# An RWKV pass: lora's second products as 64-row tiles in one place, y in one bank, turn steps at full width, normalisation in the next scan

## The reference, cut to what matters

```python
h = jnp.concatenate([x, dx], axis=-1) @ w_comb
r, k, v, g, w_lo, a_lo = jnp.split(h, ...)            # 2048 wide each; w_lo and a_lo are 64 wide
w = -jax.nn.softplus(-(w0 + jnp.tanh(w_lo) @ w2)) - 0.5
a = jax.nn.sigmoid(a0 + a_lo @ a2)
...
y = _wkv7_scan(r, decay, k, v, -kk, kk * a)           # a recurrence over tokens, a 64 x 64 state per head
mean, var = ...                                       # of y, over a head's 64
y = ((y - mean) * lax.rsqrt(var + GN_EPS)).reshape(B, L, D_INNER)
y = y * ln_w + ln_b
y = (y + bonus) * jax.nn.silu(g)
return y @ w_out
```

## Time and profile before

| | us |
|---|---|
| three runs | 2237.74, 2241.88, 2242.10 (median 2241.88) |
| the profiled execution | 2238.95 |
| its span in the profile | 2237.2 |
| passes 0 to 17 on PE | from about 753 to about 1680 |
| one full pass (scan to scan) | 54.23 |

### The profile page before, as it was taken

How to read it: one execution, slowest core, us unless ns; L and a number is a source line. 1 busy time by engine, 2 the same in 40 slices (tenths; PEclk the granted TensorE clock), 3 DMA queues, 4 the chain that set the end, 5 groups by cost and what they waited for, 6 DMA issues and landing times.

```text
span 2237.2 us, 51106 instructions
## 1 busy us (share of the span) xinstructions
PE 2205.0 (99%) x21595; PEld 1783.4 (80%) x21595; DVE 1262.2 (56%) x2442; ACT 838.3 (37%) x1725; POOL 1156.3 (52%) x802
## 2 busy tenths in 40 slices
PE   8999999999999999999999999999999999999998
PEld 7888888788888677777777777777789788888877
DVE  5465467877730955555555555656550376656621
ACT  4122212333310445555555555555421334434311
POOL 5555567787766263444444444444636444444454
PEclk9999999999999999999999999999999999999999
DMA  3323233333332222222222222222523332212132
GB/s 117 95 76 85 76 95 94 94 95 96 103 105 85 63 84 60 70 80 70 70 80 79 80 72 70 70 72 79 188 62 100 111 79 64 60 48 64 53 131 85
DMA packets 262107, 188.02 MB, mean 84 GB/s; under 512 B 18283, under 2 KB 242409, under 8 KB 261497
## 3 DMA queue, kind: packets, MB, share of 16 engines
q1 hardware_dynamic: 261881, 184.76, 27.6%
HBM read 162.69 MB, written 22.04 MB: 83 GB/s over the span
## 4 chain that ended last, share of the span: by engine, by line
PE 93%; DVE 3%; POOL 1%; ACT 1%; issue 1%; DMA 0%; SPq 0%; DVEq 0%; POOLq 0%; ACTq 0%
PE ps L1415 21%; PE ps L161 16%; PE ps L162 15%; PE ps L163 15%; PE ps L1601 3%; PE ps L1617 3%; PE ps L1643 2%; PE ps L1590 2%; PE ps L2561 1%; PE ps L1428 1%; PE ps L1557 1%; PE ps L226 1%; PE ps L1529 1%; PE ps L1546 1%; PE ps L1579 1%; PE ps L1515 1%
## 5 line engine op out<-in xcount | busy, mean ns | idle before, releaser
L152 POOL TENSOR_TENSOR w_lo<-raw,w_hi 128x1024 fp32r<-128x1024 f32 (+1 forms) x164 | 418.7, 2553 | 13.7
L149 POOL TENSOR_SCALAR w_hi<-raw 128x1024 fp32r<-128x1024 f32 (+1 forms) x164 | 182.8, 1114 | 438.8 <-PE ps L163 424.1
L161 PE MATMUL ps<-h_hi,w_hi 128*128 128x512 f32 x616 | 243.0, 395 | 4.0 <-DVE h_lo L936 2.3
L163 PE MATMUL ps<-h_hi,w_lo 128*128 128x512 f32 x616 | 240.9, 391 | 0.0
L162 PE MATMUL ps<-h_lo,w_hi 128*128 128x512 f32 x616 | 240.8, 391 | 0.0
L1415 PE MATMUL ps<-mixed_k,raw 128*64 128x264 f32 x1024 | 149.3, 387 | 0.0
L1415 PE MATMUL ps<-mixed_r,raw 128*64 128x264 f32 x1024 | 143.9, 387 | 0.0
L161 PEld LDWEIGHTS ps<-h_hi,w_hi 128*128 128x128 f32 x616 | 116.4, 189 | 29.3 <-DVE h_lo L1119 2.8
L1415 PE MATMUL ps<-mixed_g,raw 128*64 128x264 f32 x1024 | 138.3, 386 | 0.0
L163 PEld LDWEIGHTS ps<-h_hi,w_lo 128*128 128x128 f32 x616 | 116.2, 189 | 24.8
L162 PEld LDWEIGHTS ps<-h_lo,w_hi 128*128 128x128 f32 x616 | 116.4, 189 | 23.2
(11 more groups left out here) (477 smaller groups left out, 6008.5 us busy)
## 6 DMA issues: line engine op xcount, KB each, us to landing
raw<-in_rwkv_w_in_dram SPq DMA_DIRECT2D x64, 512.0 KB, 4.1
raw<-in_w_up_dram SPq DMA_DIRECT2D x44, 512.0 KB, 3.8
raw<-in_w_in_dram SPq DMA_DIRECT2D x41, 512.0 KB, 3.9
raw<-in_w_down_dram SPq DMA_DIRECT2D x22, 512.0 KB, 3.6
raw<-in_mla_w_in_dram SPq DMA_DIRECT2D x22, 512.0 KB, 4.0
sb_kept<-xT SPq DMA_DIRECT2D x16, 528.0 KB, 2.7
xT<-sb_kept SPq DMA_DIRECT2D x16, 528.0 KB, 4.7
raw<-in_rwkv_w_out_dram SPq DMA_DIRECT2D x16, 512.0 KB, 3.6
```

The source lines that it names most:

```text
L149: nc.gpsimd.tensor_scalar(w_hi[s][:, 0:width], raw[s][:, 0:width], 1.0, 0.0, ALU.mult, ALU.add).then_inc(split_hi, 1)
L152: nc.gpsimd.tensor_tensor(w_lo[s][:, 0:width], raw[s][:, 0:width], w_hi[s][:, 0:width].bitcast(F32), ALU.subtract).then_inc(split_ready, 1)
L161: nc.tensor.matmul(dst, w[0], x[0], start=start, stop=False)
L163: return nc.tensor.matmul(dst, w[1], x[0], start=False, stop=stop)
```

## The change

1. **Lora.** `wz` becomes `wa_rows`, 128 x 128: w's 64 rows above a's. Two memsets on DVE go. A new `lora_products` makes all four products in one piece, w0, a0, w1, a1, each one product on a 64-row tile, into banks 1, 7, 4 and 6 (from column 64). It is one step, the fourth of a pass (after `LORA_LEAD` = 3 steps of r0; in pass 0 after 7), and waits for the last `a_ev` of the pass before and for the bonus's eviction. `ITEMS` has w0, a0, w1, a1 first. There are 64 + 1 steps.
2. **Fills.** `FILL_END` is 0, the first chunk's fills are (1, 2, 1). In chunk 0 the first fill runs before the wait for `tl_ev`, not behind the products of line 1538.
3. **y** of chunks 0 to 7 lies in bank 5, of chunk 8 in bank 6; ACT evicts 512 and 64 columns where it had 256 and 320.
4. **Turn.** The two steps of `FILL_TURN` are one product each over the array's full width (`wide`).
5. **Normalisation.** For passes 2 to 14 (`deferred`) DVE's multiplication is cut in two halves and moved into chunk 1 of the next pass's scan, ACT's `gn_affine` behind its items of chunk 2. z and its write follow; SP's `load_sums` goes behind the load of v's weights.

```diff
-wz = raw[0][:, KD * P:KD * P + 2 * P].rearrange("p (a b) -> p a b", a=2)
+wa_rows = raw[0][:, KD * P:KD * P + P]
...
-SCAN_FILLS = [(1, 2, 2)] + [(1, 1, 2)] * (NC_ - 2) + [(1, 1, 2)]
-FILL_TURN, FILL_GRAM, FILL_FIRST, FILL_END = 2, 7, 4, 2
+SCAN_FILLS = [(1, 2, 1)] + [(1, 1, 2)] * (NC_ - 1)
+FILL_TURN, FILL_GRAM, FILL_FIRST, FILL_END = 2, 7, 4, 0
...
-ITEMS = [("r", 0), ("w", 0), ("a", 0), ("r", 1), ("w", 1), ("a", 1), ("k", 0), ("k", 1),
+ITEMS = [("w", 0), ("a", 0), ("w", 1), ("a", 1), ("r", 0), ("r", 1), ("k", 0), ("k", 1),
          ("v", 0), ("v", 1), ("g", 0), ("g", 1)]
-ITEM_BANK = [{"w": 4, "a": 7}.get(kind, h) for kind, h in ITEMS]
-SCAN_ITEMS = {1: (0,), 2: (1, 2), 4: (3,), 5: (4, 5), 7: (6,)}
-
...
+LORA = 4
+LORA_LEAD = 3
+ITEM_AT = [(1, 0), (7, 0), (4, 0), (6, C)] + [(h, 0) for _, h in ITEMS[LORA:]]
+SCAN_ITEMS = {1: (0, 1), 2: (2,), 3: (3, 4), 4: (5,), 6: (6,)}
+
+def item_out(n):
+    bank, at = ITEM_AT[n]
+    return ps[:, bank, at:at + T2 // 2]
+
+def deferred(i):
+
+    return 2 <= i < PAIRS - 1
+
+def projection(pe, i, n, wide):
...
+    dst = item_out(n)
+    t = "rkvg".index(kind)
...
+        ge(pe, a_ev, 12 * i - 1)
+    if h == 0:
...
+    for k in range(KD):
+        if i == 0 and h == 0:
...
+        for m in ([slice(0, P)] if wide[0] else own):
+            mm = nc.tensor.matmul(dst[m, :], raw_k[t % 2][:, k, m], mixed[t][:, k, cols], start=(k == 0), stop=(k == KD - 1))
...
         yield
+
+def lora_products(pe, i):
+
+    pe.wait_ge(s_wa, 32 * i + 32)
+    if i == 0:
+        pe.wait_ge(lora_ev, 2 * KD + 2)
+        pe.wait_ge(cst2, CONSTANTS)
+    else:
+        pe.wait_ge(a_ev, 12 * i)
+        pe.wait_ge(fa, 14 * i + (FA["bon"] - 14))
+    for n in range(LORA):
+        kind, h = ITEMS[n]
+        rows = own["wa".index(kind)]
+        nc.tensor.matmul(item_out(n), wa_rows[rows, :], wa_in[rows, h * (T2 // 2):(h + 1) * (T2 // 2)],
+                         start=True, stop=True).then_inc(a_mm, 1)
+
+def a_steps(pe, i, wide):
+
+    first = projection(pe, i, LORA, wide)
+    yield from itertools.islice(first, LORA_LEAD if i else KD - 1)
+    lora_products(pe, i)
+    yield
+    yield from first
+    for n in range(LORA + 1, len(ITEMS)):
+        yield from projection(pe, i, n, wide)
...
-        return ps[:, 5 + n % 2, C * (n // 2):C * (n // 2) + C]
+        return ps[:, 5 + n // 8, C * (n % 8):C * (n % 8) + C]
...
                 ge(pe, gn_ln, c)
             if n == 0:
+                if A:
+                    fill(links[n][0])
                 pe.wait_ge(tl_ev, 6 * c + 6)
+            if n == NC_ - 1 and A:
+                pe.wait_ge(a_ev, 12 * i + LORA)
             for h in range(2):
-                nc.tensor.matmul(y_at(n)[own[h], :], uv[:, n, h, :], rb[:, n, own[h]], start=True, stop=False)
+                nc.tensor.matmul(y_at(n)[own[h], :], uv[:, n, h, :], rb[:, n, own[h]], start=(n % 8 == 0), stop=False)
...
-        fill(links[n][0])
+        if n or not (A and Cs):
+            fill(links[n][0])
...
-            pe.wait_ge(a_ev, 12 * i + 5)
+            pe.wait_ge(a_ev, 12 * i + LORA)
...
         if A or i == PAIRS:
+            wide[0] = True
             fill(fill_turn)
+            wide[0] = False
...
-            if q == 2 and A:
-                pe.wait_ge(a_ev, 12 * i + 6)
...
+        act.wait_ge(a_mm, 12 * i + (LORA if n < LORA else n + 1))
...
+    def gn_affine(c):
+        act.wait_ge(yn_ev, 2 * c + 2)
+        nc.scalar.activation(yb_b, yn_b, ACT.Identity, scale=prm_at("ln_w", c), bias=prm_at("ln_b", c)).then_inc(yb_ev, 1)
...
-                ge(act, yn_ev, c)
-                nc.scalar.activation(y_c[:, C:9 * C].rearrange("p (j b) -> p j b", b=2 * C)[:, :, 0:C],
-                                     ps[:, 6, 0:4 * C].rearrange("p (j b) -> p j b", b=C), ACT.Copy).then_inc(yy_ev, 1)
+                ge(act, yn_ev, 2 * c)
+                nc.scalar.activation(y_c[:, 0:8 * C], ps[:, 5, :], ACT.Copy).then_inc(yy_ev, 1)
                 act.wait_ge(yy_mm, 2 * c + 2)
-                nc.scalar.activation(chunks(y_c)[:, 0:NC_:2, :], ps[:, 5, 0:5 * C].rearrange("p (j b) -> p j b", b=C),
-                                     ACT.Copy).then_inc(yy_ev, 1)
+                nc.scalar.activation(y_c[:, 8 * C:TP], ps[:, 6, 0:C], ACT.Copy).then_inc(yy_ev, 1)
...
+        if n == 2 and deferred(i - 1):
+            gn_affine(c - 1)
...
+    if Cs and not deferred(i):
+        gn_affine(c)
...
-    dve.wait_ge(a_ev, 12 * i + 5)
+    dve.wait_ge(a_ev, 12 * i + 3)
...
-    for h in range(2):
-        nc.vector.memset(wz[own[1 - h], h, :], 0.0).then_inc(pads, 1)
...
+    def normalised(c, parts):
+        dve.wait_ge(gn_r, c + 1)
+        ge(dve, z_pool, 4 * c)
+        for p in parts:
+            at = slice(p * (T2 // 2), (p + 1) * (T2 // 2))
+            nc.vector.tensor_tensor(yn_b[:, at], token_cols(y_c, p), ysq_b[:, at], ALU.mult).then_inc(yn_ev, 1)
...
         for n in range(NC_):
             dve.wait_ge(p_mm, 9 * c + (n + 1))
             nc.vector.tensor_copy(p_sb[:], ps[:, 2, 0:C]).then_inc(p_ev, 1)
+            if n == 1 and deferred(i - 1):
+                normalised(c - 1, (0,))
             dve.wait_ge(u_mm, 9 * c + (n + 1))
             for h in range(1 if n else 2):
                 nc.vector.tensor_copy(uv[own[h], n, h, :], ps[own[h], 2, C:P]).then_inc(u_ev, 1)
+            if n == 1 and deferred(i - 1):
+                normalised(c - 1, (1,))
             if n < NC_ - 1:
                 if n == 0:
...
-    if Cs:
-        dve.wait_ge(gn_r, c + 1)
-        ge(dve, z_pool, 4 * c)
-        nc.vector.tensor_tensor(yn_b, y_c[:, PAD:TP], ysq_b, ALU.mult).then_inc(yn_ev, 1)
+    if Cs and not deferred(i):
+        normalised(c, (0, 1))
...
-    if Cs:
-        ge(sp, z_pool, 4 * c)
-        sp.wait_ge(s_sbk, 16 * c + 16)
-        sp.dma_start(sb_c, sb_kept[ds1(c), :, :, :].rearrange("a p b n -> p (a b) n")).then_inc(s_sbl, 16)
+    if Cs and not A:
+        load_sums(sp, c)
...
-        next_weights(0, 4, 2, i)
+        next_weights(0, 6, 2, i)
+        if Cs:
+            if deferred(i - 1):
+                keep_z(sp, c - 1)
+            load_sums(sp, c)
         if i == 1:
             keep_sums(sp, 0)
         if not last:
-            sp.wait_ge(a_mm, 12 * i + 6)
+            sp.wait_ge(a_mm, 12 * i + LORA)
...
-    if Cs and c < READY:
-        sp.wait_ge(z_pool, 4 * c + 4)
-        sp.dma_start(z_kept[ds1(c), :, :, :].rearrange("a p b n -> p (a b) n"), z_hl[:].bitcast(F32)).then_inc(s_zk, 16)
+    if Cs and c < READY and not deferred(i):
+        keep_z(sp, c)
```

More of the change, by code:

```diff
@@ L1386, in token_cols @@
             return buf[:, PAD + h * (T2 // 2):PAD + (h + 1) * (T2 // 2)]
-        ITEMS = [("r", 0), ("w", 0), ("a", 0), ("r", 1), ("w", 1), ("a", 1), ("k", 0), ("k", 1),
+        ITEMS = [("w", 0), ("a", 0), ("w", 1), ("a", 1), ("r", 0), ("r", 1), ("k", 0), ("k", 1),
                  ("v", 0), ("v", 1), ("g", 0), ("g", 1)]
-        ITEM_BANK = [{"w": 4, "a": 7}.get(kind, h) for kind, h in ITEMS]
-        SCAN_ITEMS = {1: (0,), 2: (1, 2), 4: (3,), 5: (4, 5), 7: (6,)}
-        def a_products(pe, i, n):
+        LORA = 4
@@ L1396, in a_products @@
+        LORA_LEAD = 3
[7 more added lines that the diff above has]
+        def projection(pe, i, n, wide):
             kind, h = ITEMS[n]
-            bank = ITEM_BANK[n]
+            dst = item_out(n)
+            t = "rkvg".index(kind)
@@ L1398, in a_products @@
             cols = slice(h * (T2 // 2), (h + 1) * (T2 // 2))
-            dst = ps[:, bank, 0:T2 // 2]
-            before = [m for m in range(n) if ITEM_BANK[m] == bank]
+            before = [m for m in range(n) if ITEM_AT[m][0] == h]
             if before:
                 pe.wait_ge(a_ev, 12 * i + (before[-1] + 1))
[L1403 to L1419, removed]
-            else:
[L1421 to L1429, removed]
-                yield
@@ new lines, in projection @@
+            else:
+                ge(pe, a_ev, 12 * i - 1)
+            if h == 0:
+                pe.wait_ge(rw_landed[t % 2], 32 * i + (16 * (t // 2) + 16))
+            for k in range(KD):
+                if i == 0 and h == 0:
+                    pe.wait_ge(mx_done, KD * t + k + 1)
+                for m in ([slice(0, P)] if wide[0] else own):
+                    mm = nc.tensor.matmul(dst[m, :], raw_k[t % 2][:, k, m], mixed[t][:, k, cols], start=(k == 0), stop=(k == KD - 1))
+                if k == KD - 1:
+                    mm.then_inc(a_mm, 1)
+                yield
@@ L1495, in pass_pe @@
             b, c = i - 1, i - 2
-            steps = itertools.chain.from_iterable(a_products(pe, i, item) for item in (range(12) if A else []))
+            wide = [False]
+            steps = a_steps(pe, i, wide) if A else iter(())
             if i >= PAIRS:
@@ L1509, in y_at @@
             def y_at(n):
-                return ps[:, 5 + n % 2, C * (n // 2):C * (n // 2) + C]
+                return ps[:, 5 + n // 8, C * (n % 8):C * (n % 8) + C]
             def y_new(n):
                 for h in range(2):
```

(26 more changed lines are left out.)

## The result

The changed kernel takes 2245.73 us (median of 16 runs, 2241.93 to 2262.75) against 2240.37 (16 runs, 2237.32 to 2242.38): ratio 1.0044, interval 1.0026 to 1.0063. The ratio is that of the means here; the medians are 5.4 us or 0.24% apart. The kernel is slower, where 2232 was forecast. Its runs fall in two groups, eleven at 2241.9 to 2246.2 (median 2244.41, 4.0 above before) and five at 2259.9 to 2262.8. The five make up more than half of what the means differ by. The profiled execution is one of the second group.

A forecast was written before the change was run, and what follows sets the result against it. PE was taken to bound the kernel. 14 passes x (0.36 + 0.13) = 6.86, plus 0.46 for passes 0 and 1, gave 7.3 us off 2238.95, called 2232 us; range 2226 to 2239.

The forecast's parts named there:

- Bound: Whole kernel: PE, busy 2205.0 of 2237.2 us, sets the time; other engines count only where PE waits.
- prices: PE's instructions: a step takes 0.445 us, full width costs the same, and row tiles work side by side.
- lora: Lora products on PE: 1.78 us removed, 0.89 and 0.30 added, saving 0.59 a pass without a new wait.
- new wait: Lora waits for ACT's copy of g1: stall 0.44 us, chunk 1's p at T + 3.28, 0.36 saved a pass.
- end of pass: Chunk 0's y and DVE's multiplication around the end of a pass: no wait, nothing gained or lost.
- Rival 1: Lora's wait for g1's copy is absent or hidden: 0.78 us saved a full pass, 2226.7 us; chance 0.10.
- Rival 3: Lora's row tiles don't work side by side: 0.40 us lost a pass, 2245.9 us; chance 0.09.
- Turn: Steps between transposes and gram products: full width removes a change of shape, 0.13 us saved a pass.
- Rival 4: Full-width steps at the turn show their weight loads: 2245.0 us; chance 0.03.
- Normalisation: Deferred DVE halves of about 0.36 us fit chunk 1's gaps, gn_affine fits chunk 2: cost 0.
- Rival 2: Deferred work overhangs in the scan's chain, 0.14 us at three places, 0.42 a pass: 2237.1 us; chance 0.18.
- Passes 0 and 1: First two passes: 0.59 us saved in pass 0, -0.13 in pass 1 after a 1.00 stall, together 0.46.

The follow-up runs named there:

- experiment 9: Experiment 2 with the turn's full-width steps put back into column halves: 2233.80 us, ratio 0.9980 to the kernel before.
- experiment 2: Changed kernel with the deferred halves in chunk 3, gn_affine in chunk 4, and the multiplications of passes 15 to 17 in one piece: 2233.00 us, ratio 0.9969.
- experiment 5: Experiment 4 with GpSimd's last four products of a pass waiting until DVE has done both deferred halves: 2232.74 us, ratio 0.9975.
- experiment 8: Changed kernel with DVE's multiplication back at the end of the pass in one piece, only gn_affine deferred: 2236.25 us, ratio 0.9990.
- experiment 4: Changed kernel with the undeferred multiplication of passes 15 to 17 in one piece again: 2243.52 us, ratio 1.0018.
- experiment 6: Kernel before with DVE's multiplication at the end of each pass cut in two halves, same place: 2250.85 us, ratio 1.0053.
- experiment 10: Experiment 2 with lora two steps later, between p and u of chunk 1: 2233.49 us, ratio 0.9973.
- experiment 11: Experiment 2 with lora as chunk 1's last fill, behind s, w0 evicted in chunk 1, a0 and w1 in chunk 2: 2227.39 us, ratio 0.9957.
- experiment 7: Experiment 2 with the multiplications of passes 15 to 17 in two halves again: 2234.48 us, ratio 0.9992.

## Why the prediction was wrong

- **Bound, prices, lora, new wait, end of pass:** right for passes 2 to 15. Row tiles overlap (the lora group takes 1.09 of 0.89 + 0.30, part of the shape change falling into the wait), p of chunk 1 came at T + 3.31 for 3.28. Rivals 1 and 3 fall by the same rows.
- **Turn:** right, 0.14 (experiment 9) to 0.16 for 0.13. Rival 4 falls.
- **Normalisation:** this is the step that failed. "In chunk 1 DVE idles 0.57 before u and 0.52 before the state: both fit", and "Cost 0." I took the halves' length from the row of 0.71, in which DVE had started 0.19 before GpSimd's product, and looked at DVE's gaps alone. The other side of it stood in GpSimd's timeline of the kernel before: its product took 1.79 beside DVE's multiplication, and 1.41 where DVE did nothing:

```profile
791.24 1.41 POOL L2007 TENSOR_TENSOR rkv<-kk_b,e_ex 128x576 f32<-128x576 f32 x1
...
1159.63 1.79 POOL L2007 TENSOR_TENSOR rkv<-kk_b,e_ex 128x576 f32<-128x576 f32 x1
```

  In chunk 1 GpSimd is in the middle of an instruction each time. Measured: +0.81 a pass (54.57 against 53.76), 13 passes, 10.5 us. A half takes 0.42 even when GpSimd is quiet, not 0.36; that alone cost nothing (experiments 2 and 5). ACT's part of the step was right: `gn_affine` fits in chunk 2, and having it out of lora's way is worth 0.53 a pass (experiment 8). Rival 2 had the right place with the wrong mechanism and half the size (0.42). Without the collision the sum stands: experiment 5 is 6.1 us below the kernel before, where 7.3 was forecast.

  The Trainium skill says it (SBUF — State Buffer, "SBUF: two separate sides"): a DVE operation with two SBUF inputs and a GpSimd instruction that reads SBUF share a pair of ports, and the first one holds it to its end. The trace agrees: 1.00 and 1.40 beside GpSimd, 0.42 without it. With the measured 0.81 a pass the sum would have been 2231.6 + 10.5 = 2242.1, 3.2 above the 2238.95 that it started from: no gain, in place of one of 7.
- **One piece or two** was not weighed at all. At the end of pass 15 it costs 1.3 (57.34 against 56.06), and in some executions 15 more, by the clock: 72.50 - 57.34 = 15.2. Another 0.23 of pass 16 (56.06 against 55.83) is in its chunk 0; I had put 0. With the end fills gone p follows the bonus at once, and DVE's 0.71 ends only at 1597.13 in experiment 4, 0.82 behind the start of p, so that p's copy waits for it.
- **Passes 0 and 1:** 0.46 forecast, 0.00 measured. The stall in pass 1 was as forecast (1.02), and pass 1 is 0.2 longer for a forecast 0.13. Pass 0 gave 0.23 of its 0.59: the nine steps of r behind lora take 4.37 there, where nine steps at 0.445 make 4.01. Why is open.

Passes 2 to 15 give +3.76 and pass 16 +1.5 without the clock's fall, together 5.3. The eleven executions without it lie 4.0 above the kernel before, so 1.3 is not accounted for; the runs of one group spread over 4 to 5 us. The median of all sixteen lies 5.4 above, but it takes in the five of the upper group, and that it meets the sum is chance.

## What to carry to other kernels

A gap on an engine is room for an operation only if the operation is as long there as in the row that it is priced from: for DVE with two SBUF operands look at what GpSimd runs in that window, and add what is left of that instruction. Don't cut such an operation in two where GpSimd has its next instruction ready (experiment 6). When you put a big piece of independent work into a chain whose results come just in time, the place behind the product whose result comes latest (here s) was the best of the three tried (experiments 2, 10 and 11).

## What was not expected of the hardware

- A DVE operation of 264 columns takes 0.42 alone and up to 1.64 beside GpSimd; GpSimd's 1.41 becomes 1.79 when DVE is first.
- In one profiled execution an idle PE of 1.38 us was followed by 37.55 us at 1.2 GHz, 15 us of the time; in another profiled one it was followed by nothing. By their times two of 11 and five of 16 executions are of the first kind. Whether the multiplication of passes 15 to 17 is cut in two was all that the variants differed in (experiments 2 and 7, and 4 and the changed kernel); why some executions are spared is open.
- Putting lora's row tiles between column halves costs PE 0.33 us for both changes of shape: in experiment 11 chunk 1 takes 2.90 with lora and two steps. With four steps it took 2.57; lora's 0.89 stands in for two of them, and 0.33 is left over. With full-width steps behind the transposes, in place of column halves, the way to the gram products is 0.14 shorter (2.03 for 2.17).
